# Last down projection in column halves, first casts in halves, last scatter in 128-column blocks: a two-layer hybrid trunk with a routed MoE on one core

## The reference

```python
for l in range(DEPTH):
    h = rms_norm(x, norm1_g[l])
    z = jnp.einsum("bsd,de->bse", h, w_in[l]) + b_in[l]
    ...
    x = x + merged @ w_out[l]
    x = x + hier_moe(rms_norm(x, norm2_g[l]), w_router_group[l], w_router_expert[l],
                     w_expert_gate[l], w_expert_up[l], w_expert_down[l])
return rms_norm(x, norm_f_g)

def hier_moe(h, w_rg, w_re, w_gate, w_up, w_down):
    ...
    hg = jnp.einsum("nd,edf->nef", t, w_gate)
    hu = jnp.einsum("nd,edf->nef", t, w_up)
    a = jax.nn.silu(hg) * hu * combine[..., None].astype(t.dtype)
    return jnp.einsum("nef,efd->nd", a, w_down).reshape(b, s, d)
```

## Time and profile before

| what | us |
|---|---|
| median of 3 runs | 1040.03 |
| lowest, highest | 1038.58, 1040.14 |
| the profiled execution | 1038.1 |
| its span, first to last instruction | 1036.4 |
| PE busy (matmuls) | 963.7 |
| DVE busy, ACT busy | 576.0, 426.2 |
| mean granted clock of PE | 0.979 of full speed |

### The profile page before, as it was taken

The page is one execution under the profiler, slowest core; times in us unless marked ns, Lnnn a source line. Parts: engine busy times, 40 slices in busy tenths (PEclk is TensorE's granted clock), DMA queues, the critical chain, the costliest instruction groups (busy, mean ns, idle before and its releaser), DMA issues.

```text
span 1036.4 us, 15414 instructions
## 1 busy us (share of the span) xinstructions
PE 963.7 (93%) x5902; PEld 670.8 (65%) x5902; DVE 576.0 (56%) x1186; ACT 426.2 (41%) x907; POOL 58.4 (6%) x74
## 2 busy tenths in 40 slices
PE   8999999999999995896999999999999999878877
PEld 7788877777887441542588887777788954334323
DVE  6766788886883231130176668898869543222212
ACT  5434556666443210110363355666664431111122
POOL 1120400000010000000003004000000100000000
PEclk9999999999999999898999999999999999989989
DMA  9965543237999999999998655332589999999996
GB/s 346 347 229 191 194 129 122 82 111 263 398 362 377 419 427 419 424 423 426 415 391 282 202 183 182 123 122 82 160 293 370 378 403 414 425 422 424 425 423 273
DMA packets 97114, 313.04 MB, mean 302 GB/s; under 512 B 13424, under 2 KB 18576, under 8 KB 74512
## 3 DMA queue, kind: packets, MB, share of 16 engines
q1 hardware_dynamic: 96704, 312.04, 79.2%
q10 hardware_dynamic: 336, 0.02, 0.0%
HBM read 310.20 MB, written 1.84 MB: 301 GB/s over the span
## 4 chain that ended last, share of the span: by engine, by line
PE 66%; DMA 15%; DVE 7%; SPq 6%; ACT 3%; issue 2%; DVEq 0%; POOLq 0%; ACTq 0%
PE ps L1381 14%; PE ps L1383 13%; PE ps L1382 13%; SPq L481 6%; DMA arena<-in_w_expert_up_dram 5%; PE ps L1981 5%; DMA arena<-in_w_expert_gate_dram 3%; DMA ring_rest<-in_w_expert_down_dram 3%; DMA ring_rest<-in_w_expert_up_dram 2%; PE ps L1956 2%; DMA arena<-in_w_expert_down_dram 2%; PE ps L1501 2%; PE ps L2055 2%; PE ps L1406 2%; PE ps L1509 2%
## 5 line engine op out<-in xcount | busy, mean ns | idle before, releaser
L1381 PE MATMUL ps<-whi,ahi 128*128 128x512 f32 (+1 forms) x736 | 285.0, 387 | 4.4 <-DVE wlo L1065 3.7
L1065 DVE TENSOR_TENSOR wlo<-arena,whi 128x512 fp32r<-128x512 f32 (+1 forms) x352 | 234.4, 705 | 91.1 <-ACT whi L875 88.7
L1383 PE MATMUL ps<-whi,alo 128*128 128x512 f32 (+1 forms) x736 | 277.1, 376 | 0.0
L1382 PE MATMUL ps<-wlo,ahi 128*128 128x512 f32 (+1 forms) x736 | 276.8, 376 | 0.0
L875 ACT CAST whi<-arena 128x1024 fp32r<-128x1024 f32 (+1 forms) x176 | 180.6, 1028 | 184.6 <-PE ps L1383 177.8
L1381 PEld LDWEIGHTS ps<-whi,ahi 128*128 128x128 f32 x736 | 138.5, 188 | 35.5 <-DVE wlo L1065 8.5
L1383 PEld LDWEIGHTS ps<-whi,alo 128*128 128x128 f32 x736 | 138.4, 188 | 26.0
L1382 PEld LDWEIGHTS ps<-wlo,ahi 128*128 128x128 f32 x736 | 138.7, 188 | 23.0
L1981 PE MATMUL ps<-arena,rows 128*32 128x512 f32 x416 | 92.9, 629 | 6.1 <-DMA arena<-in_w_expert_up_dram 3.5
L2186 DVE SCALAR_TENSOR_TENSOR acts<-ps,wslot,acts 128x256 f32<-128x256 f32 x16 | 7.7, 484 | 161.5 <-ACT acts L1891 138.2
L1981 PE MATMUL ps<-ring_rest,rows 128*32 128x512 f32 x352 | 78.8, 654 | 14.9 <-DMA arena<-in_w_expert_up_dram 12.1
(11 more groups left out here) (284 smaller groups left out, 1066.4 us busy)
## 6 DMA issues: line engine op xcount, KB each, us to landing
arena<-in_w_in_dram SPq DMA_DIRECT2D x62, 1024.0 KB, 5.3
arena<-in_w_expert_down_dram SPq DMA_DIRECT2D x38, 1024.0 KB, 20.4
arena<-in_w_expert_gate_dram SPq DMA_DIRECT2D x34, 1024.0 KB, 25.9
arena<-in_w_expert_up_dram SPq DMA_DIRECT2D x32, 1024.0 KB, 26.1
ring_rest<-in_w_expert_down_dram SPq DMA_DIRECT2D x24, 1024.0 KB, 17.5
ring_rest<-in_w_expert_gate_dram SPq DMA_DIRECT2D x22, 1024.0 KB, 25.9
ring_rest<-in_w_expert_up_dram SPq DMA_DIRECT2D x22, 1024.0 KB, 26.0
arena<-in_w_proj_a_dram SPq DMA_DIRECT2D x8, 1024.0 KB, 5.3
```

The costliest lines, as they stand in the source:

```text
L1065: dve.tensor_tensor(wlo[:, jj % 2, cols], half_slot(jj, w)[:, cols], whi[:, jj % 2, cols].bitcast(F32), ALU.subtract).then_inc(low_split i ...
L1381: pe.matmul(o, hi, rhs_hi, start=first, stop=False)
L1382: pe.matmul(o, hi, rhs_lo, start=False, stop=False)
L1383: return pe.matmul(o, lo, rhs_hi, start=False, stop=last)
```

## The change

1. **The last expert's down weights** come in two transfers of 512 columns with all 256 rows, in place of two transfers of 128 rows with all 1024 columns. Each partition's 4 KB piece becomes two pieces of 2 KB. `down_last` makes, for each expert, columns 0 to 511 first and then 512 to 1023, in blocks of 128 columns in place of 256 (64 matmul calls of 128 columns in place of 32 of 256 for a layer). The first half of y is complete one transfer earlier. The last `keep_clock` behind it is gone.
2. **The split of y.** ACT casts the first half only. DVE subtracts for the first half, then casts the second half itself and subtracts (new semaphore `y_high_odd`).
3. **The last scatter** follows the blocks of 128 columns: `scatter_quarter` now issues 8 matmuls with 128 moving columns in place of 4 with 256, so 32 in place of 16 for a layer. In layer 1's trunk each quarter waits for the low parts that it needs in place of all of them.
4. **The first cast of each layer** is made in two halves (`first_high`, semaphores `hi_first` and `hi_ready`). In layer 1 the casts of the transposed x stand ahead of and between the two halves; before, the whole cast stood ahead of them. DVE makes `alo` ahead of `wlo` for the first three steps of both layers.
5. **Layer 0's start.** The transpose of the second gain vector (one small matmul) moves on PE from ahead of the first step to ahead of step j = 2; DVE's copy of it moves one step later. Some semaphores are merged (masks in and out; second gains and positions), which leaves every issue of a transfer at its place.

The diff, cut to what the steps below speak of:

```diff
-            for kf in range(2):
-                sp.dma_start(slot[:, kf * D:(kf + 1) * D], src[:, kf * D:(kf + 1) * D]).then_inc(last_in[1 + kf], 16)
+            to, src = (t.rearrange("p (k d) -> p k d", k=2) for t in (slot, src))
+            for nh in range(2):
+                cols = slice(nh * BANK, (nh + 1) * BANK)
+                sp.dma_start(to[:, :, cols], src[:, :, cols]).then_inc(last_in[1 + nh], 16)
...
         Y_PARTS = (y_hi, y_lo)
 
         def st_last(c):
 
             n = QUADS - 1
-            return (st_r[:, n % 2, :], st_turned[:, 0, :], st_turned[:, 1, :], st_r[:, 1 - n % 2, :])[c]
+            return (st_r[:, n % 2, :], st_turned[:, 0, :], st_turned[:, 1, :], st_r[:, 1 - n % 2, :])[c % 4]
 
         def scatter_quarter(pe, q, first):
 
             tb, nh = q % 2, q // 2
             for part in Y_PARTS:
-                for i in range(2):
-                    c = 2 * nh + i
-                    mm = pe.matmul(ps[:, 4 + q, i * CQ_W:(i + 1) * CQ_W], st_last(c)[:, tb * P:(tb + 1) * P],
-                                   part[:, c * CQ_W:(c + 1) * CQ_W], start=first and part is y_hi and i == 0,
+                for i in range(4):
+                    c = 4 * nh + i
+                    mm = pe.matmul(ps[:, 4 + q, i * P:(i + 1) * P], st_last(c)[:, tb * P:(tb + 1) * P],
+                                   part[:, c * P:(c + 1) * P], start=first and part is y_hi and i == 0,
                                    stop=part is y_lo, skip_group_check=True)
             return mm
...
-                        def x_high(pairs):
+                        def x_high(pairs, odds=(0, 1)):
                             for i in pairs:
                                 act.wait_ge(turned, i + 1)
-                                for k in (2 * i, 2 * i + 1):
+                                for k in [2 * i + odd for odd in odds]:
                                     act.activation(ahi[:, k, :], ps[:, 4 + i, (k % 2) * S:(k % 2) * S + S], ACT.Copy,
                                                    scale=first_gain(l, k)).then_inc(turned_hi, 1)
+
+                        def first_high(kk, done):
+                            cols = slice(kk * BANK, (kk + 1) * BANK)
+                            act.copy(whi[:, 0, cols], half_slot(0, BANK)[:, cols]).then_inc(done, 1)
 
...
                         else:
                             act.wait_ge(before_me.gu_ready, QUADS)
                         for j in range(8):
+                            if j == 0:
+                                x_high((0,), (0,) if l else (0, 1))
+                                act.wait_ge(first_in, 16)
+                                first_high(0, hi_first)
+                                if l:
+                                    x_high((0,), (1,))
+                                first_high(1, hi_ready)
+                                if l:
+                                    x_high((1,))
+                                continue
                             if l == 0 and j < 3:
                                 x_high((j,) if j < 2 else (2, 3))
-                            if j == 0:
-                                act.wait_ge(first_in, 16)
-                            high(j, BANK, 16 if j else None, j - 1 if j >= 2 else None)
-                            if l and j < 2:
-                                x_high((2 * j, 2 * j + 1))
+                            high(j, BANK, 16, j - 1 if j >= 2 else None)
+                            if l and j == 1:
+                                x_high((2, 3))
...
                         for j in range(8):
-                            if l == 0 and j < 3:
+                            if j < 3:
                                 x_low(range(2 * j, 2 * j + 2) if j < 2 else range(4, KB))
-                            if l and j < 2:
-                                for kk in range(2):
-                                    low_half(j, BANK, j + 1, kk)
-                                    x_low(range(4 * j + 2 * kk, 4 * j + 2 * kk + 2))
-                            else:
-                                low(j, BANK, j + 1)
-                            if l == 0 and j == 2:
+                            low(j, BANK, j + 1, hi_ready if j else hi_first)
+                            if l == 0 and j == 3:
                                 dve.wait_ge(gains_ready, 2)
                                 dve.tensor_copy(gains[:, DEPTH * KB:], ps[:, 2, 0:DEPTH * KB]).then_inc(gains_done, 1)
...
-                            pe.wait_ge(gain2_in, 16)
-                            turn_gains(1, 2)
...
-                            pe.wait_ge(hi_ready, j + 1)
                             for kk in range(2):
+                                if j == kk == 0:
+                                    pe.wait_ge(hi_first, 1)
+                                else:
+                                    pe.wait_ge(hi_ready, j + 1)
                                 both(kk, (turned_hi, 2 * j + kk + 1), ahi, whi)
...
                         for j in range(8):
+                            if l == 0 and j == 2:
+                                pe.wait_ge(gain2_pos_in, 32)
+                                turn_gains(1, 2)
                             if l == 0 and j == 4:
                                 pe.wait_ge(gains_done, 2)
                             if l and j == 2:
-                                pe.wait_ge(turned_lo, KB)
-                                scatter_last(pe, before_me)
+                                for q in range(4):
+                                    pe.wait_ge(turned_lo, 2 * (q + 1))
+                                    scatter_quarter(pe, q, True).then_inc(before_me.back_ready, 1)
...
                     if n == LAST and not routed:
                         act.copy(y_hi[:, 0:BANK], ps[:, 2, :]).then_inc(y_high, 1)
-                        act.wait_ge(R.y_ready, 2 * n + 2)
-                        act.copy(y_hi[:, BANK:2 * BANK], ps[:, 3, :]).then_inc(y_high, 1)
...
-                            if e == 3 and kf:
+                        for nh in range(2):
+                            if e == 3 and nh:
                                 keep_clock(pe, 1, 0)
-                            if e == kf == 0:
+                            if e == nh == 0:
                                 pe.wait_ge(last_two_in, 32 * (l + 1))
-                            elif e == 3 or e == 2 and kf == 0:
-                                pe.wait_ge(last_in[e - 2 + kf], 16 * (l + 1))
-                            for c in range(4):
-                                g = (e + c) % 4
-                                mm = pe.matmul(ps[g * EC:(g + 1) * EC, 2 + c // 2, (c % 2) * CQ_W:(c % 2 + 1) * CQ_W],
-                                               at_sb[:, kf, e * EC:(e + 1) * EC], w[:, kf * D + c * CQ_W:kf * D + (c + 1) * CQ_W],
-                                               start=(kf == 0), stop=(kf == 1), skip_group_check=True)
-                                if e == 3 and kf and c % 2:
-                                    mm.then_inc(R.y_ready, 1)
-                    keep_clock(pe, 1, 0)
+                            elif e == 3 or e == 2 and nh == 0:
+                                pe.wait_ge(last_in[e - 2 + nh], 16 * (l + 1))
+                            for kf in range(2):
+                                for c in range(4):
+                                    g = (e + c) % 4
+                                    at = kf * D + nh * BANK + c * P
+                                    mm = pe.matmul(ps[g * EC:(g + 1) * EC, 2 + nh, c * P:(c + 1) * P],
+                                                   at_sb[:, kf, e * EC:(e + 1) * EC], w[:, at:at + P],
+                                                   start=(kf == 0), stop=(kf == 1), skip_group_check=True)
+                            if e == 3:
+                                mm.then_inc(R.y_ready, 1)
...
                     for nh in range(2):
-                        for part, made in ((y_hi, y_high), (y_lo, y_low)):
-                            pe.wait_ge(made, 2 * l + nh + 1)
+                        for part in Y_PARTS:
+                            if part is y_lo:
+                                pe.wait_ge(y_low, 2 * l + nh + 1)
+                            else:
+                                pe.wait_ge(y_high_odd if nh else y_high, l + 1)
                             for k in range(4 * nh, 4 * nh + 4):
-                                mm = pe.matmul(turned_part(k), part[:, k * P:(k + 1) * P], st_last(k // 2),
+                                mm = pe.matmul(turned_part(k), part[:, k * P:(k + 1) * P], st_last(k),
                                                start=False, stop=part is y_lo, skip_group_check=True)
                                 if part is y_lo and k % 2:
...
                         for nh in range(2):
                             cols = slice(nh * BANK, (nh + 1) * BANK)
-                            dve.wait_ge(y_high, 2 * l + nh + 1)
```

(4 more changed lines are left out.)

35 lines of the change are left out of this document (15 added, 20 removed).

## The result

| | us |
|---|---|
| before, median of 22 runs | 1038.67 (1037.55 to 1041.73) |
| after, median of 22 runs | 1041.1 (1038.48 to 1044.16) |
| ratio after to before | 1.0022, 95% interval 1.0015 to 1.0028 |
| span of the profiled execution, before and after | 1036.4, 1041.6 |

The change makes the kernel slower by 0.22%, about 2.3 us (1.6 to 2.9). Of the 5.2 us between the two profiled spans only 2.4 lie at the passage and at the end: 1.5 us are there by the first convolution of layer 0, most of it in the transposes of x, and 1.1 us come between the passage and the last down calls of layer 1. Kernels whose code is the same there differ by as much between their profiles.

A forecast was written before the change was run, and what follows sets the result against it. PE was taken as the bound (66% of the chain, busy 93% of the span). Terms -0.45 - 0.28 + 1.87 + 0.57 = +1.7 us on a median of 1040.03 gave 1041.7 us, range 1038.8 to 1044.0.

The forecast's parts named there:

- start of layer 0: Layer 0's first step: the half cast lets PE start at 8.49 in place of 8.95; -0.45 us.
- transfers in 2 KB pieces, both places: Expert 3's weight halves, both layers: smaller pieces flow slower, 0.11 us more for each half; +0.44 us in all.
- passage without scatter, from the second half's start: Passage to layer 1: earlier first half and split of y win more than ACT's new order loses; -0.50 us.
- scatter in layer 0: Passage to layer 1: 32 matmuls at 0.117 us, set by the weight load, nothing hides it; +1.87 us.
- end, from the second half's start: Layer 1's end: PE's narrower scatter calls set the last square; +0.35 us without the slower transfer.
- the low bound: Scatter at the passage: a 128-column call costs 0.110 us, making the scatter +1.64 us.
- Rival A: Scatter, passage and end: narrow fp32r columns cost more, about 0.21 us a call; sum +7.1 us, 1047.1; chance 0.12.
- Rival B: Scatter, passage and end: narrow calls cost in proportion, 0.058 us; sum -0.9 us, 1039.1; chance 0.09.
- taken as the same 0.67: Last down calls at the passage: 0.67 us from last landing to cast, though 8 calls of 128 columns replace 4.
- The wait for ACT's new order: Layer 1's first step: PE's third matmul waits for ACT's second half cast; 0.36 us lost.
- Rival C: Passage: late `turned` delays both half casts, losing 0.5 us in place of gaining 0.28; 1042.5; chance 0.11 with another rival.
- hidden by 0.37 us of idle time ahead of j = 4: Layer 0's start: the moved transpose costs PE 0.13 us ahead of j = 2, covered by later idle time.

The follow-up runs named there:

- e2: Kernel before with only layer 0's start changed: first cast in two halves, second gain transpose moved behind step 1, merged semaphores; 1037.53 us, ratio 0.9991.
- e7: Kernel before with the last scatter of each layer in 64-column pieces, 64 matmuls in place of 16; 1056.94 us, ratio 1.0164.
- e6: Kernel after with eight unread small matmuls (sixteen passes) on PE ahead of a layer's last transposes; 1040.19 us, ratio 1.0018.
- e4: Kernel after with both half casts of layer 1's weights ahead of the casts of x again; 1039.77 us, ratio 1.0018.
- e11: Kernel before with column halves, 256-column blocks, first cast in two halves; second gain transpose ahead of the first step, waiting for its own rows alone; 1038.76 us, ratio 1.0005.
- e12: Kernel after with casts ahead, eight small matmuls, and second gain transpose ahead of the first step, waiting for its own rows alone; 1040.15 us, ratio 1.0016.
- e8: Kernel before with column halves in 256-column blocks, layer 0's first cast in two halves and the gain transpose moved; 1038.58 us, ratio 0.9995.
- e5: Kernel after with two unread small matmuls (four passes) on PE ahead of a layer's last transposes; one profile, 1042.16 us.
- e1: Kernel before with only the last scatter in 128-column blocks, 32 matmuls in place of 16; 1040.53 us, ratio 1.0023.

## Why the prediction was right in size, and where its steps failed

The forecast was +1.7 us and the kernel lost 2.3 (1.6 to 2.9). The main mechanism stands: the passage's scatter is on the path, nothing hides it, and its price is the weight load's. That the sum came so near is in part luck: the passage without the scatter was missed by 1.05 us, and the other four terms were off by 0.1 to 0.4 each, three of them to the other side. The time given, 1041.7, stood on a median of three runs that 22 runs put 1.4 us lower. The terms:

| term | predicted | measured | from |
|---|---|---|---|
| start of layer 0 | -0.45 | -0.1 | the table of e2 |
| transfers in 2 KB pieces, both places | +0.44 | 0.0 | time between the landings of the halves, all profiles |
| passage without scatter, from the second half's start | -0.50 | +0.55 | 13.07 - 10.88 - 1.64 |
| scatter in layer 0 | +1.87 | +1.64 | 3.52 - 1.88 |
| end, from the second half's start | +0.35 | +0.22 | 5.12 - 4.90 |
| sum | +1.7 | +2.3 | |

**The scatter.** I took 0.117 us a call although the nearest row for the load said 0.110, and the low bound was the truth, at 128 and at 64 columns. Rival A (0.21 us) falls: the price appears only in e7, and there it comes with the halved clock, behind calls of the same width that cost 0.111. Rival B falls too; with it the Trainium skill's page "TensorE: Matmul & The Clock Gate", whose section "Back-to-back issue gap" gives 81 ns for 128 columns. Here it is 110. The same page's section "LDWEIGHTS (loading the stationary operand)" has P / 1.2 ns with P the columns of the weights, an estimated 107 ns for 128 columns, and with this the trace agrees.

**The passage.** The step that failed is the last down calls, "taken as the same 0.67" us: from their start to the cast of the second half it took 1.53 us, and 0.75 with the stop moved off the path (e6). The sum had layer 1's first step 2.68 us behind that start; it came at +3.58, and at +2.79 in e6. The wait for ACT's new order, 0.36 by the sum, was 0.39 (0.84 between the pairs for 0.45 due), and e4 takes it away. These two eat what the early half wins. Behind the first step the sum held: 5.97 us to the scatter for 5.82. Rival C named what happened, down calls that end late and so a late `turned`, with the right sign, but not this cause.

**The start.** The 0.46 us is there at the first step (0.42) and gone by the fourth. Two steps failed. The moved transpose was taken as hidden by 0.37 us of idle time ahead of j = 4, but it stands ahead of j = 2, where PE had none. And I asked only whether ACT and PE were ready earlier, not when the second weights land: the cast that follows waits 0.56 us for them in e2. The trace of the kernel before had this too: there they land at 9.66 and the cast starts at 9.68. Which of the two eats the gain depends on how early PE starts: the transfers where the transposes of x are fast (e11), the moved transpose otherwise (e6 against e12). The 0.9 us that e2 shows by its times (0 to 1.8) is more than the marks explain, and e8 and e11, which have the first half cast too and the column halves beside it, don't show it.

**The transfers.** 2 KB pieces cost nothing that shows, not 0.11 us a half. In the ten kernels with them the halves land 1.26 to 1.29 us apart in layer 0 and 1.24 to 1.28 in layer 1 (but for the late one in e4); in the four with 4 KB pieces 1.26 to 1.31 and 1.23 to 1.24. The GB/s of a stretch with other traffic in it was a poor price for these.

**The end.** The early quarter and PE's pace at the third and fourth square came as told. Column halves are worth most here: the scatter alone makes the end 0.97 us longer, the whole change 0.22.

## What to carry to other kernels

A matmul with its own 128 x 128 fp32r weights costs 0.11 us from 32 to 128 columns and 0.117 at 256, so splitting a 256-column call in two nearly doubles it; count such calls first, and look where the split spreads to (here the scatter inherits the down projection's blocks). A head start at a place that streams its operands is worth only what the next transfer allows: look for the landing behind the one that you make ready earlier. With 64 calls of 64 columns in a row the clock joined the price. And two repairs on one path are not to be added up before asking what is ready next: here it was a transfer.

## What the runs showed of the hardware

**Calls that hardly do more than load weights can lower the clock.** A PE busy without a gap, with 64 columns for each load, went from 2.4 to 1.2 GHz in the middle of its scatter (e7); with 128 columns for each load no passage did.

**PE can stop at a fixed place of its stream.** 0.39 to 0.50 us between two matmuls (0.65 to 0.71 between two weight loads), while transfers ran at 397 to 399 GB/s (after, e5). In the three profiles that show it, a transfer of 16 KB on an instruction queue starts 1.8 to 2.0 us before the stop. That fits a PE that waits for its instructions, but its packet was done about 0.9 us before the stop, and other kernels have such transfers without a stop, so what holds PE isn't shown. Nor was it tried whether the queues' traffic matters. In layer 1's end no stop shows.

**The same start, several speeds.** The 16 transposes of x took 1.97 us in six profiles, 2.18 to 2.75 in five and 3.67 in three, with the same code ahead of them. The trace's records of the granted clock account for it: one transpose follows the other by 0.21 us ahead of the first record and by 0.11 behind it. In the kernel before the spacing changes at 7.2 us, in e12 at 6.9, where their records begin. The records begin, at full speed, at 5.1 to 5.9 us, ahead of or within the first transposes, in the six fast profiles; at 6.3 (2.18 us) and 6.9 (2.38 us); at 7.2 to 7.7 in the three that took 2.61 to 2.75; and at 10.7 to 11.3, behind the last transpose, in the three slow ones (`after`, e1, e5). Before its first record a trace says nothing of the clock, and a window there reads 1.00. The Trainium skill's page "TensorE: Matmul & The Clock Gate" (section "What's actually happening") says that the moment of the rise varies from run to run, by about 0.5 us either way; the traces agree that it varies, over 6 us.

**A collision that an early start avoids.** A pass of POOL starts at 22.4 to 22.9 us in every profile, when its weights land. Where DVE's two subtractions for step 5 begin by 21.97 they take 1.29 us (six profiles); begun at 21.99 to 22.37 they run beside POOL and take 2.64 (three), and begun later still they are slower or come behind it. First the profile of e2, then that of e6:

```profile
21.53 1.29 DVE L1068 TENSOR_TENSOR wlo<-arena,whi 128x512 fp32r<-128x512 f32 x2
22.64 1.59 POOL L798 TENSOR_SCALAR_AFFINE_SELECT probs<-probs 128x1536 f32<-128x1536 f32 x1 [19.66 <-DMA probs<-in_w_spatial_dram]
```

```profile
21.99 2.64 DVE L1073 TENSOR_TENSOR wlo<-arena,whi 128x512 fp32r<-128x512 f32 x2
22.47 1.62 POOL L795 TENSOR_SCALAR_AFFINE_SELECT probs<-probs 128x1536 f32<-128x1536 f32 x1 [19.48 <-DMA probs<-in_w_spatial_dram]
```

PE then waits 0.3 us in the three and 1.0 to 1.2 in the later ones, and not at all in the six. So a start that is late by a few tenths can cost up to a microsecond more, which may be part of the spread between runs and of e2's 0.9 us; that share wasn't measured. The Trainium skill's page "GPSIMD Engine Reference" (section "Specifications") says that POOL shares its SBUF interfaces with DVE and that they contend where a DVE instruction has two SBUF inputs; these have, and the rows agree.
